# First pair of projection tiles as eight block products, and forget-rank products between the products of a pair

## The chip, the core and the metric

The kernel runs on one core of a Trainium2 chip. The metric is the time of one execution on the device in microseconds (us), the median of several. The core's engines work in parallel and each takes its instructions in program order: TensorE (PE in the profile, its weight loads PEld), VectorE (DVE), ScalarE (ACT), GpSimd (POOL) and SyncE (SP), which here issues the DMA transfers.

## What is computed

One mixer layer on 1,088 tokens (1,024 of a prompt, 64 of a running stream), width 2,048, all in fp32:

```
u = rms_norm(h, norm_pre)
qa, ka, va, za, qg, kg, vg, zg, lr, ga, gg = split_cols(u @ w_in)
y_a = (banded_attention(qa, ka, va) * silu(za)) @ w_branch_attn
log_a = log_sigmoid(lr @ w_forget_up + b_forget) / GLA_TAU
y_g = (rms_norm(gla_mix(qg, kg, vg, log_a, state), gla_norm) * silu(zg)) @ w_branch_gla
merged = sigmoid(ga + b_a) * y_a + sigmoid(gg + b_g) * y_g
h = h + rms_norm(merged @ w_out, norm_post)
```

The change is in `u @ w_in`. The tokens x are multiplied by `norm_pre`, the products are made of these, and the per-token root (rstd) is multiplied onto the results.

## The kernel before

**Numbers.** An fp32 product is made of three fp32r products: of each operand a "hi" part (a copy in the format fp32r, by ScalarE) and a "lo" part (the rest, raw minus hi, by VectorE) are made, and TensorE adds hi*hi, hi*lo and lo*hi in PSUM.

**The mixing phase.** The columns of `w_in` are 60 tiles of 128 (44 of the projections, 16 of the gates), taken two at a time: 30 pairs on the token group 544 to 1087, then the same 30 on tokens 0 to 543. `n` counts these 60 pairs, and pair 30 is `TURN`, where the token group changes. A pair is a 2x2 block problem (2 tiles, 2 halves of the contraction of 8 blocks of 128 rows, 2 halves of 272 tokens: `GAW`), done by a Strassen-like scheme with 7 products (`N_Q`, `q` 0 to 6) in place of 8, of sums of weight blocks (`sum_weights`, four per pair, VectorE) and of sums of token blocks. A product (`split_product`, L1756) is 24 matmuls of 128x272. The weights' hi parts are made by `hi_mix` (L862) into a ring of 3, their lo parts by `lo_mix` (L1206). The results of the products are taken out of PSUM banks 0 to 2 by ScalarE (`s1`, L906) and VectorE (L1339 to L1403, c11, c12, c21, c22), which signal `s_post`; TensorE waits for that before it writes a bank again. TensorE signals each product by `s_mp`.

**The start.** Before pair 0, a loop over 8 steps `j` handles the tokens: each x transfer brings 2 blocks x 544 tokens (rows of 2,176 bytes). ScalarE squares them (L873, into `lr`, with two slots), and TensorE sums the squares over the partitions (L1786: the squares are the weights, a column of ones is moved, 10 matmuls a step in the program, each shown as two). ScalarE and VectorE scale the four blocks (L875, L1236), VectorE forms the four combinations (L1242 to L1248), and every second step ScalarE makes 7 hi parts (L888) and VectorE 7 lo parts (L1253) of 544 elements. Pair 0 waits for the last of these (`s_tlo`). The roots are made during pair 0: mean (L1274), power -0.5 on GpSimd (L1144), diagonals (L1281), a product that spreads them over partitions (L1749), a copy (L1293).

**Forget-rank products.** `lr_products` (L1766) multiplies tokens by the 16 columns of lr (hi and lo as 32 weight columns), as 80 matmuls of 128x272 into banks 4 and 5, in two sums: of 2 terms for one token half and 3 for the other, each term 16 matmuls. It stands after pair 0 and after `TURN`:

```
            for n in range(MIX):
                for q in range(N_Q):
...
                if n == 0:
                    pe.wait_ge(s_lrlo, 1)
                if n % MIX_PAIRS == 0:
                    lr_products()
```

**Second token group.** In pairs 2 to 9 VectorE also combines the tokens of the other group (`held`, L1376 to L1381) and SP stores them; in pairs 29 and 30 they are loaded again (`load_held`) and split by ScalarE (L919) and VectorE (`lo_held`, L1300), between that pair's own work. After the mixing phase come forget gates, late gates with attention and linear attention between their products, the branch products and the output products; nothing there is touched by the change. SP issues all transfers in one queue, in the order written (`load_mix`, `x_first`, `store_mix`, `x_second`, `store_held`).

## Time and profile before

| | |
|---|---|
| median of 3 runs | 2900.48 us (2900.36 to 2903.83) |
| the profiled execution | 2900.14 us, of which the span is 2898.4 us |
| TensorE busy | 2792.8 us, 96% |
| VectorE busy | 1990.5 us, 69% |
| ScalarE busy | 1164.4 us, 40% |
| TensorE clock granted, mean | 0.992 of full |

In the profile, the engine lines give time in which an instruction ran. In the timeline a row has a start in us, how long it ran, engine, line and operation, what it wrote and read (buffer numbers left out), how often, and in brackets the idle time before it and what ended it. Matmuls overlap: the distance of two starts is what one costs the stream, the duration contains its way through the array.

### The profile page before, as it was taken

What the parts mean: (1) busy time and instruction counts of PE and PEld (TensorE: products, weight loads), DVE (VectorE), ACT (ScalarE), POOL (GpSimd) and SP (SyncE); (2) the same over time, 40 slices, a digit from 0 to 9 for tenths busy, and PEclk for the clock granted to TensorE, in tenths of its full rate; (3) what the DMA queues carried; (4) which work ended last, traced back from release to release, by engine and by line L of the source; (5) the groups of instructions that cost most, each with busy time, mean ns of one, the idle gap of its engine ahead of it and who ended that gap; (6) DMA issues with size and microseconds to landing.
All of it is one profiled execution on the core that took longest, in us unless ns stands there. A gap on an engine that the chain in (4) does not pass through costs nothing.

```text
span 2898.4 us, 51546 instructions
## 1 busy us (share of the span) xinstructions
PE 2792.8 (96%) x20490; PEld 2654.8 (92%) x20490; DVE 1990.5 (69%) x3171; ACT 1164.4 (40%) x1908; POOL 80.7 (3%) x55
## 2 busy tenths in 40 slices
PE   6999999999899999999999999999899999999996
PEld 6999999999899999999777887877799999999996
DVE  6799777777788777777777777787543333555555
ACT  5333333344354333344566566565420000343331
POOL 0122000000000000000000000000000000000001
PEclk9999999999999999999999999999999999999998
DMA  3455333435344343433656665565553333555564
GB/s 120 133 182 189 128 129 118 133 125 202 113 133 134 126 130 120 130 122 126 190 176 180 181 188 173 163 195 162 183 169 114 116 115 125 177 179 190 182 192 142
DMA packets 227619, 441.00 MB, mean 152 GB/s; under 512 B 24272, under 2 KB 135120, under 8 KB 226528
## 3 DMA queue, kind: packets, MB, share of 16 engines
q1 hardware_dynamic: 227424, 438.31, 47.4%
q8 instruction: 134, 2.20, 0.3%
q14 instruction: 61, 0.50, 0.0%
HBM read 358.10 MB, written 80.67 MB: 151 GB/s over the span
## 4 chain that ended last, share of the span: by engine, by line
PE 38%; issue 6%; DVE 4%; DMA 2%; ACT 2%; POOL 0%; SPq 0%; POOLq 0%; ACTq 0%; DVEq 0%
PE bank L1734 31%; PE bank L1931 1%; PE bank L1892 1%; DVE w_lo L1185 1%; PE bank L1951 1%; PE bank L1875 1%; PE bank L1956 1%; PE bank L1958 1%; DMA ring<-o_scratch 1%; DVE s L1452 1%; PE bank L1862 1%; ACT w_hi L839 1%; PE bank L1910 0%; DMA ring<-m_scratch 0%; DVE bl L1562 0%
## 5 line engine op out<-in xcount | busy, mean ns | idle before, releaser
L1756 PE MATMUL bank<-th,w_hi 128*128 128x272 f32 x2400 | 699.1, 291 | 14.5 <-DVE w_lo L1206 7.8
L1756 PE MATMUL bank<-tl,w_hi 128*128 128x272 f32 x2400 | 694.1, 289 | 0.0
L1756 PE MATMUL bank<-th,w_lo 128*128 128x272 f32 x2400 | 693.6, 289 | 0.0
L839 ACT ACTIVATE w_hi<-w_raw 128x1024 fp32r<-128x1024 f32 x256 | 270.7, 1058 | 677.6 <-PE bank L1734 638.8
L1185 DVE TENSOR_TENSOR w_lo<-w_raw,w_hi 128x1024 fp32r<-128x1024 f32 x256 | 313.2, 1223 | 250.9 <-ACT w_hi L839 250.5
L1756 PEld LDWEIGHTS bank<-th,w_hi 128*128 128x128 f32 x2400 | 452.7, 189 | 19.8 <-DVE w_lo L1206 10.8
L1756 PEld LDWEIGHTS bank<-tl,w_hi 128*128 128x128 f32 x2400 | 452.8, 189 | 1.0 <-issue 1.0
L1756 PEld LDWEIGHTS bank<-th,w_lo 128*128 128x128 f32 x2400 | 452.3, 188 | 0.0
L862 ACT ACTIVATE w_hi<-w_more 128x1024 fp32r<-128x1024 f32 x240 | 254.6, 1061 | 475.5 <-DVE w_more L1225 255.2
L1206 DVE TENSOR_TENSOR w_lo<-w_more,w_hi 128x1024 fp32r<-128x1024 f32 x240 | 301.4, 1256 | 125.3 <-ACT w_hi L862 123.0
L1734 PE MATMUL bank<-uh,w_hi 128*128 128x272 f32 x1024 | 316.0, 309 | 11.3 <-DVE w_lo L1185 6.4
L1734 PE MATMUL bank<-uh,w_lo 128*128 128x272 f32 x1024 | 295.9, 289 | 0.0
L1734 PE MATMUL bank<-ul,w_hi 128*128 128x272 f32 x1024 | 295.5, 289 | 0.0
L1756 PE MATMUL bank<-uh,w_hi 128*128 128x272 f32 x960 | 280.8, 292 | 5.0 <-ACT stage L906 4.4
L1756 PE MATMUL bank<-ul,w_hi 128*128 128x272 f32 x960 | 279.5, 291 | 0.0
L1756 PE MATMUL bank<-uh,w_lo 128*128 128x272 f32 x960 | 279.0, 291 | 0.0
L862 ACT ACTIVATE w_hi<-w_raw 128x1024 fp32r<-128x1024 f32 x180 | 189.7, 1054 | 195.6 <-PE bank L1756 194.8
L1734 PE MATMUL bank<-bh,w_hi 128*128 128x362 f32 (+1 forms) x768 | 253.7, 330 | 9.0 <-DVE bl L1562 6.8
L1734 PE MATMUL bank<-mh,w_hi 128*128 128x362 f32 (+1 forms) x768 | 252.4, 329 | 1.7 <-DVE ml L1191 1.7
L1734 PE MATMUL bank<-bh,w_lo 128*128 128x362 f32 (+1 forms) x768 | 252.8, 329 | 0.0
L1734 PE MATMUL bank<-bl,w_hi 128*128 128x362 f32 (+1 forms) x768 | 252.6, 329 | 0.0
L1734 PE MATMUL bank<-mh,w_lo 128*128 128x362 f32 (+1 forms) x768 | 252.1, 328 | 0.0
(205 smaller groups left out, 4999.7 us busy)
## 6 DMA issues: line engine op xcount, KB each, us to landing
w_raw<-in_w_tiles SPq DMA_DIRECT2D x376, 512.0 KB, 4.0
w_more<-in_w_tiles SPq DMA_DIRECT2D x120, 512.0 KB, 3.3
p_scratch<-stage SPq DMA_DIRECT2D x44, 544.0 KB, 3.0
gate<-gate_scratch SPq DMA_DIRECT2D x32, 544.0 KB, 4.0
gl<-p_scratch SPq DMA_DIRECT2D x24, 512.0 KB, 5.2
gate_scratch<-stage SPq DMA_DIRECT2D x16, 544.0 KB, 3.0
gate_scratch<-stage SPq DMA_DIRECT2D x64, 136.0 KB, 4.0
o_scratch<-ob SPq DMA_DIRECT2D x16, 512.0 KB, 5.2
```

The source lines that it names most:

```text
L839: act.activation(w_hi[:, h], w_raw[:, h], ACT.Copy).then_inc(s_whi, 1)
L862: act.activation(ring_hi[done % RING], w_src_of[RAW_OF[q]], ACT.Copy).then_inc(s_phi, 1)
L1185: dve.tensor_tensor(w_lo[:, h], w_raw[:, h], w_hi[:, h].bitcast(f32), ALU.subtract).then_inc(s_wlo, 1)
L1206: dve.tensor_tensor(ring_lo[done % RING], w_src_of[RAW_OF[q]], ring_hi[done % RING].bitcast(f32), ALU.subtract).then_inc(s_plo, 1)
L1452: ins = dve.tensor_tensor_reduce(out=s8[0:nq, u % 2, i, 1 + lo:1 + hi], in0=bank[u % 2][0:nq, :].rearrange("p (i k) -> p i k", i=2)[:, i, ...
L1734: ins = pe.matmul(out[:, 0:w], wt[:, h, k, :], ut[:, h * HK + k, 0:w], start=start and k == 0 and j == 0, stop=stop and k == HK - 1 and j ...
L1756: ins = pe.matmul(out[:, 0:GAW], wt[:, k], ut[:, k], start=start and k == 0 and i == 0, stop=stop and k == HK - 1 and i == 2, skip_group_c ...
L1862: ins = pe.transpose(dst[0:nk[kt], kt, i, 0:nq], pb[0:nq, u % 4, i, 1 + kt * P:1 + kt * P + nk[kt]], ident[0:nq, 0:nq])
L1875: ins = pe.matmul(bank[half][0:nq, :].rearrange("p (i k) -> p i k", i=2)[:, i, c0:P + nq], qa[r, tile + i, 0:nq], kw[r, tile // 4, c0:P + ...
L1892: ins = pe.matmul(bank[3][half * HEAD_DIM:(half + 1) * HEAD_DIM, :].rearrange("p (j q) -> p j q", j=GROUP)[:, :, 0:nq], v[0:nk[kt], g * HE ...
L1931: ins = pe.matmul(bank[4][r, l * CHUNK:(l + 1) * CHUNK], k, q, start=True, stop=True)
L1951: ins = pe.matmul(bank[(5, 1)[c]][:, 0:GLA_DV], kt_tok[r, hh], vg[r, v], start=True, stop=True)
```

## The change

It replaces the start and pair 0, moves parts of pair 1's preparation, and moves the forget-rank products.

- Pair 0 is made of eight plain block products (`FIRST`, `first_product`), of two weight tiles x two contraction halves x two token halves, each needing only one raw weight block and one raw token block. Results land in banks 0 to 3, one per quarter.
- x comes as eight transfers of 4 blocks x 272 tokens (rows of 1,088 bytes). A token block is scaled (VectorE three, ScalarE one), and its hi and lo parts are made in halves of 1,088 elements.
- Squares go in 16 pieces into four slots of two blocks; `first_ones` sums a piece by two fp32 matmuls with 64 columns of ones as weights and the squares moved (128x272), one into partitions 0 to 63, one into 64 to 127 of bank 6 or 7. They stand between the block products. After the last, ScalarE copies both banks to `lr` and a `token_sums` (5 matmuls of one column) finishes the sum; the root chain then follows, behind pair 0 and no longer within it.
- The four token combinations are made after the block parts (`sum_blocks`), their hi and lo parts (`hi_sum`, `lo_sum`) partly between pair 1's weight parts.
- `lr_products` is cut up: the two terms of the first sum behind pair 0 (in `TURN` after q=2), two terms of the second after q=4 and the third after q=6 of pair 1 and of `TURN`.

The diff's core:

```
--- before.py
+++ after.py
@@ -43,7 +43,14 @@
-X_FIRST = 5
+FIRST_BLOCKS = ((0, 0), (0, 1), (1, 0), (1, 1))
+FIRST = ((0, 0), (1, 0), (0, 1), (1, 1), (2, 2), (2, 3), (3, 2), (3, 3))
+FIRST_SUMS = (1, 3, 4, 5)
+TOK = 16
+LR_AT = (1, TURN)
...
-                if n > 0:
+                if n == 1:
+                    sp.wait_ge(s_plo, (4, 6, 5, 7)[what])
+                elif n > 1:
                     if what == 0:
-                        sp.wait_ge(s_sum, 4 * (n - 1) + 3)
+                        sp.wait_ge(s_sum, 4 * (n - 2) + 3)
                     else:
                         sp.wait_ge(s_plo, N_Q * (n - 1) + (7, 4, 6)[what - 1])
                 sp.dma_start(w_src_of[slot], w_src(row, h)).then_inc(s_wr[what], 16)
 
+            def x_first(b, half):
+
+                kh, th = FIRST_BLOCKS[b]
+                k, a = kh * HK + 4 * half, MIX_GROUPS[0] * MIX_W + th * GAW
+                sp.dma_start(x_block[b][half], x_view[:, k:k + 4, a:a + GAW]).then_inc(s_x[2 * b + half], 16)
+
+            x_first(0, 0)
+            x_first(0, 1)
             load_mix(0, 0)
-            x_first(2)
-            x_first(3)
             load_mix(0, 2)
+            x_first(1, 0)
+            x_first(1, 1)
+            x_first(2, 0)
+            x_first(2, 1)
+            load_mix(0, 1)
+            x_first(3, 0)
+            x_first(3, 1)
             load_mix(0, 3)
-            x_first(4)
-            x_first(5)
-            load_mix(0, 1)
-            x_first(6)
-            x_first(7)
...
+            def hi_first(e):
+
+                act.wait_ge(s_wr[(0, 2, 1, 3)[e]], 16)
+                ge(act, s_mp, e + 1 if e == 3 else 0)
+                act.activation(ring_hi[(3 + e) % RING], w_src_of[(0, 2, 1, 3)[e]], ACT.Copy).then_inc(s_phi, 4 if e == 0 else 1)
+
+            def squares(*pieces):
+
+                for i in pieces:
+                    b, k = i // 4, 2 * (i % 4)
+                    act.wait_ge(s_x[2 * b + k // 4], 16)
+                    ge(act, s_psq, i - 3)
+                    act.activation(sq_slot[i % 4], x_block[b][k // 4][:, k % 4:k % 4 + 2], ACT.Square).then_inc(s_sq1, 1)
+
+            def hi_block(b):
+
+                for half in range(2):
+                    c = slice(4 * half, 4 * half + 4)
+                    if b == 2:
+                        act.wait_ge(s_xa1, half + 1)
+                    else:
+                        act.wait_ge(s_xgd, 2 * (0, 1, None, 2)[b] + half + 1)
+                    act.activation(block_hi[b][:, c], scaled_block[b][:, c], ACT.Copy).then_inc(s_thi, 1)
+
+            def hi_sum(i):
+
+                q = FIRST_SUMS[i]
+                for half in range(2):
+                    c = slice(4 * half, 4 * half + 4)
+                    act.wait_ge(s_tt, (4, 2, 0, 6)[i] + half + 1)
+                    act.activation(tok_hi[q][:, c], tok_raw[q][:, c], ACT.Copy).then_inc(s_thi, 1)
+
+            squares(0, 1)
+            hi_block(0)
+            hi_first(0)
+            hi_first(1)
+            squares(2, 3, 4, 5)
+            hi_block(1)
+            for half in range(2):
+                act.wait_ge(s_x[4 + half], 16)
+                for k in range(4 * half, 4 * half + 4):
+                    ins = act.activation(scaled_block[2][:, k], x_block[2][half][:, k % 4], ACT.Copy, scale=pre(HK + k))
                 ins.then_inc(s_xa1, 1)
+            hi_block(2)
+            hi_first(2)
+            squares(6, 7)
+            hi_block(3)
+            hi_first(3)
+            squares(*range(8, 16))
+            act.wait_ge(s_sq1, 16)
+            hi_sum(0)
+            act.wait_ge(s_psq, 16)
+            for half in range(2):
+                act.activation(lr[:, half * GAW:(half + 1) * GAW], bank[6 + half][:, 0:GAW], ACT.Copy).then_inc(s_sqc, 1)
+            hi_mix(1, 0)
+            hi_sum(1)
+            hi_sum(2)
+            hi_mix(1, 1)
...
+            def scale_block(b):
+
+                for half in range(2):
+                    dve.wait_ge(s_x[2 * b + half], 16)
+                    for k in range(4 * half, 4 * half + 4):
+                        ins = dve.tensor_scalar(scaled_block[b][:, k], x_block[b][half][:, k % 4], pre(FIRST_BLOCKS[b][0] * HK + k), None, ALU.mult)
+                    ins.then_inc(s_xgd, 1)
+
+            def lo_block(b):
+
+                for half in range(2):
+                    c = slice(4 * half, 4 * half + 4)
+                    dve.wait_ge(s_thi, 2 * b + half + 1)
+                    dve.tensor_tensor(block_lo[b][:, c], scaled_block[b][:, c], block_hi[b][:, c].bitcast(f32), ALU.subtract).then_inc(s_tlo, 1)
+            def lo_first(e):
+
+                dve.wait_ge(s_phi, 4 + e)
+                dve.tensor_tensor(ring_lo[(3 + e) % RING], w_src_of[(0, 2, 1, 3)[e]], ring_hi[(3 + e) % RING].bitcast(f32),
+                                  ALU.subtract).then_inc(s_plo, 4 if e == 0 else 1)
...
+            def lo_sum(i):
+
+                q = FIRST_SUMS[i]
+                for half in range(2):
+                    c = slice(4 * half, 4 * half + 4)
+                    dve.wait_ge(s_thi, 8 + 2 * i + half + 1)
+                    dve.tensor_tensor(tok_lo[q][:, c], tok_raw[q][:, c], tok_hi[q][:, c].bitcast(f32), ALU.subtract).then_inc(s_tlo, 1)
+
+            scale_block(0)
+            lo_block(0)
+            lo_first(0)
+            lo_first(1)
+            scale_block(1)
+            lo_block(1)
+            scale_block(3)
+            lo_block(2)
+            lo_first(2)
+            lo_block(3)
+            lo_first(3)
+            b11, b12, b21, b22 = scaled_block
+            dve.wait_ge(s_xgd, 6)
+            sum_blocks(b11, b12, b11)
+            sum_blocks(b12, b22, b12)
+            dve.wait_ge(s_tt, 2)
+            sum_blocks(b22, b22, b11)
+            dve.wait_ge(s_mp, 5)
+            dve.wait_ge(s_tt, 6)
+            dve.wait_ge(s_xa1, 2)
+            sum_blocks(tok_raw[5], b21, b22)
...
-            for n in range(MIX):
+            lo_mix(1, 0)
+            lo_sum(0)
+            mean_squares(0, MIX_W, bank[5], HEAD_DIM)
+            root_diagonals(0, MIX_W)
+            sum_weights(1, 1)
+            sum_weights(1, 2)
+            lo_mix(1, 1)
+            first = MIX_GROUPS[0] * MIX_W
+            spread(0, MIX_W, bank[6:8], rstd[:, first:first + MIX_W])
+            dve.wait_ge(s_rstd, 2)
+            for i, (m, half) in enumerate(((0, 0), (0, 1), (1, 0), (1, 1))):
+                dve.wait_ge(s_mp, 6 + m)
+                ins = dve.tensor_tensor(c_out[:, m, half * GAW:(half + 1) * GAW], bank[i][:, 0:GAW],
+                                        rstd[:, first + half * GAW:first + (half + 1) * GAW], ALU.mult)
+                if i < 3:
+                    ins.then_inc(s_post, (2, 3, 1)[i])
+                else:
+                    ins.then_inc(s_cm, 3)
+
...
+                if n == 1:
+                    lo_sum(1)
...
-            def lr_products():
-
-                for i, terms in enumerate((((0, 0), (1, 2)), ((0, 4), (0, 0), (1, 6)))):
...
+            def lr_products(i, which):
+
+                terms = LR_TERMS[i]
+                for n in which:
+                    kh, q = terms[n]
+                    for k in range(HK):
+                        for j, ut in enumerate((tok_hi[q], tok_lo[q])):
+                            ins = pe.matmul(bank[4 + i][0:2 * RANK, 0:GAW], wlr[:, kh * HK + k, :], ut[:, k],
+                                            start=n == 0 and k == 0 and j == 0, stop=n == len(terms) - 1 and k == HK - 1 and j == 1)
+                if which[-1] == len(terms) - 1:
                     ins.then_inc(s_lrp, 1)
...
+            def first_ones(*pieces):
+
+                for i in pieces:
+                    th = FIRST_BLOCKS[i // 4][1]
+                    pe.wait_ge(s_sq1, i + 1)
+                    for j in range(2):
+                        ins = pe.matmul(bank[6 + th][j * HEAD_DIM:(j + 1) * HEAD_DIM, 0:GAW], ones[:, 0:HEAD_DIM], sq_slot[i % 4][:, j],
+                                        start=i in (0, 4), stop=i in (11, 15), skip_group_check=True)
+                    ins.then_inc(s_psq, 1)
+
+            def first_product(n):
+
+                e, b = FIRST[n]
+                pe.wait_ge(s_plo, 4 + e)
+                hi_w, lo_w = ring_hi[(3 + e) % RING], ring_lo[(3 + e) % RING]
+                for k in range(HK):
+                    if k % 4 == 0:
+                        pe.wait_ge(s_tlo, 2 * b + k // 4 + 1)
+                    for i, (wt, ut) in enumerate(((hi_w, block_hi[b]), (hi_w, block_lo[b]), (lo_w, block_hi[b]))):
+                        ins = pe.matmul(bank[2 * (e % 2) + FIRST_BLOCKS[b][1]][:, 0:GAW], wt[:, k], ut[:, k], start=e < 2 and k == 0 and i == 0,
+                                        stop=e >= 2 and k == HK - 1 and i == 2, skip_group_check=True)
+                if FIRST_BLOCKS[b][1] == 1:
+                    ins.then_inc(s_mp, 4 if e == 0 else 1)
+
             pe.wait_ge(s_cset, 1)
-            for j in range(HK):
...
-            for n in range(MIX):
+            for n, pieces in enumerate(((0, 1), (2, 3), (4, 5), (), (), (6, 7), (8, 9, 10, 11), (12, 13, 14, 15))):
+                first_ones(*pieces)
+                first_product(n)
+            pe.wait_ge(s_sqc, 2)
+            token_sums(MIX_W, bank[5], lr)
+            pe.wait_ge(s_lrlo, 1)
+            lr_products(0, (0, 1))
+            spread_roots(0, MIX_W, bank[6:8])
+
+            for n in range(1, MIX):
                 for q in range(N_Q):
                     pe.wait_ge(s_plo, N_Q * n + q + 1)
-                    if n == 0:
-                        pe.wait_ge(s_tlo, 3 * N_Q + q + 1)
+                    if n == 1 and q in FIRST_SUMS:
+                        pe.wait_ge(s_tlo, 8 + 2 * FIRST_SUMS.index(q) + 2)
                     if n == TURN:
-                        pe.wait_ge(s_tlo, 4 * N_Q + q + 1)
+                        pe.wait_ge(s_tlo, TOK + q + 1)
...
-                if n % MIX_PAIRS == 0:
-                    lr_products()
+                    if n == TURN and q == 2:
+                        lr_products(0, (0, 1))
+                    if n in LR_AT and q == 4:
+                        lr_products(1, (0, 1))
+                    if n in LR_AT and q == 6:
+                        lr_products(1, (2,))
```

ScalarE at the start of the program, before (in program order; `lr` holds the squares, `ul_raw` and `tl_raw` the scaled and combined tokens, `uh` and `th` hi parts):

```order
L873 ACTIVATE lr<-stage 128x544 x2
L875 ACTIVATE ul_raw<-stage,norm_sb 128x272 x2
L862 ACTIVATE w_hi<-w_raw 128x1024
L873 ACTIVATE lr<-stage 128x544 x2
L875 ACTIVATE ul_raw<-stage,norm_sb 128x272 x2
L888 ACTIVATE uh<-ul_raw 128x544
L888 ACTIVATE th<-tl_raw 128x544
```

And in the changed kernel (`th_raw` and `stage` hold x, `tl_raw` and `xs` the scaled blocks):

```order
L898 ACTIVATE lr<-th_raw 128x544 x2
L908 ACTIVATE uh<-tl_raw 128x1088 x2
L890 ACTIVATE w_hi<-w_raw 128x1024
L890 ACTIVATE w_hi<-w_more 128x1024
L898 ACTIVATE ring<-th_raw 128x544 x2
L898 ACTIVATE lr<-th_raw 128x544 x2
L908 ACTIVATE th<-tl_raw 128x1088 x2
L927 ACTIVATE xs<-stage,norm_sb 128x272 x8
L908 ACTIVATE uh<-xs 128x1088 x2
L890 ACTIVATE w_hi<-w_raw 128x1024
```

One block's hi parts and the first two weights now stand right behind the first two squares; before, seven hi parts came after the second transfer and this was repeated four times.

VectorE around the roots, before (`mean` is the mean square, `ring<-ident,root` the diagonals, `rows` the spread roots, `stage` results):

```order
L1274 TENSOR_SCALAR mean<-bank 128x4
L1275 TENSOR_SCALAR mean<-bank 32x1
L1227 TENSOR_TENSOR w_more<-w_raw,w_more 128x1024
L1206 TENSOR_TENSOR w_lo<-w_raw,w_hi 128x1024
L1230 TENSOR_TENSOR w_raw<-w_raw,w_more 128x1024
L1281 TENSOR_SCALAR ring<-ident,root 128x128 x4
L1281 TENSOR_SCALAR ring<-ident,root 32x128
L1206 TENSOR_TENSOR w_lo<-w_more,w_hi 128x1024
L1339 TENSOR_TENSOR stage<-stage,bank 128x272
L1206 TENSOR_TENSOR w_lo<-w_more,w_hi 128x1024
L1293 COPY rows<-bank 128x512
```

And in the changed kernel:

```order
L1355 TENSOR_SCALAR mean<-bank 128x4
L1356 TENSOR_SCALAR mean<-bank 32x1
L1362 TENSOR_SCALAR ring<-ident,root 128x128 x4
L1362 TENSOR_SCALAR ring<-ident,root 32x128
L1277 TENSOR_TENSOR w_more<-w_more 128x1024
L1281 TENSOR_TENSOR w_more<-w_more,w_raw 128x1024
L1262 TENSOR_TENSOR w_lo<-w_more,w_hi 128x1024
L1374 COPY rows<-bank 128x512
L1374 COPY rows<-bank 128x32
L1398 TENSOR_TENSOR stage<-bank,rows 128x272 x4
```

The diagonals stand directly behind the mean, with nothing between them, and two weight sums and one weight rest of pair 1 stand between the diagonals and the copy of the spread roots.

TensorE in `TURN`, at the end of q=2, before (the product of q=3 follows at once):

```order
L1756 MATMUL bank<-uh,w_hi 128x272
L1756 MATMUL bank<-ul,w_hi 128x272
L1756 MATMUL bank<-uh,w_lo 128x272
L1756 MATMUL bank<-th,w_hi 128x272
L1756 MATMUL bank<-tl,w_hi 128x272
```

And in the changed kernel:

```order
L1855 MATMUL bank<-uh,w_hi 128x272
L1855 MATMUL bank<-ul,w_hi 128x272
L1855 MATMUL bank<-uh,w_lo 128x272
L1868 MATMUL bank<-uh,wlr 32x272
L1868 MATMUL bank<-ul,wlr 32x272
```

Thirty-two matmuls of the forget rank now stand between the products of q=2 and q=3, 32 more behind q=4 and 16 behind q=6; before, all 80 stood behind q=6.

## Rows read from the trace of the kernel before

**Rows 1.** The page, busy time of each engine (share of the span) and instructions:

```profile
PE 2792.8 (96%) x20490; PEld 2654.8 (92%) x20490; DVE 1990.5 (69%) x3171; ACT 1164.4 (40%) x1908; POOL 80.7 (3%) x55
```

**Rows 2.** Windows: length, PE, PEld, DVE, ACT, POOL busy, PEclk, DMA, GB/s:

```profile
20.00:40.00 20.00, 13.71 (x68) 13.46 (x68) 14.02 (x25) 13.29 (x25) 0.00 (x0) 1.00 0.17 46
40.00:60.00 20.00, 16.33 (x80) 16.03 (x81) 17.26 (x32) 13.15 (x24) 1.77 (x1) 1.00 0.00 1
60.00:80.00 20.00, 20.00 (x159) 19.74 (x158) 16.10 (x25) 5.91 (x7) 2.52 (x1) 1.00 0.32 107
```

**Rows 3.** Timeline of TensorE, the start:

```profile
34.32 8.03 PE L1786 MATMUL bank<-ones,lr 128*128 128x1 f32 x40 [3.07 <-ACT lr L873]
45.43 8.03 PE L1786 MATMUL bank<-ones,lr 128*128 128x1 f32 x40 [3.08 <-ACT lr L873]
54.06 0.57 PE L1756 MATMUL bank<-uh,w_hi 128*128 128x272 f32 x1 [0.60 <-DVE ul L1253]
...
59.63 0.32 PE L1756 MATMUL bank<-th,w_hi 128*128 128x272 f32 x1
```

**Rows 4.** Timeline of TensorE, end of pair 0 to first product of pair 2:

```profile
79.26 0.29 PE L1766 MATMUL bank<-uh,wlr 128*32 128x272 f32 x1
...
89.21 0.29 PE L1756 MATMUL bank<-uh,w_hi 128*128 128x272 f32 x1
...
110.40 0.29 PE L1756 MATMUL bank<-uh,w_hi 128*128 128x272 f32 x1
```

**Rows 5.** Timeline of TensorE in `TURN`, q=2 to the first product of pair 31:

```profile
734.32 0.56 PE L1756 MATMUL bank<-uh,w_hi 128*128 128x272 f32 x1 [4.41 <-ACT stage L906]
...
738.98 0.28 PE L1756 MATMUL bank<-uh,w_lo 128*128 128x272 f32 x1
...
741.46 0.36 PE L1756 MATMUL bank<-th,w_hi 128*128 128x272 f32 x1 [1.82 <-DVE stage L1339]
...
746.07 0.29 PE L1756 MATMUL bank<-th,w_hi 128*128 128x272 f32 x1
...
765.09 0.29 PE L1756 MATMUL bank<-uh,w_hi 128*128 128x272 f32 x1
```

**Rows 6.** Timeline of VectorE in `TURN`, the take-out for which q=3 waits:

```profile
738.55 2.42 DVE L1300 TENSOR_TENSOR tl<-tl_raw,th 128x2176 fp32r<-128x2176 f32 x1
740.88 0.43 DVE L1339 TENSOR_TENSOR stage<-stage,bank 128x272 f32<-128x272 f32 x1
```

**Rows 7.** Timeline of ScalarE, the start:

```profile
5.99 1.20 ACT L873 ACTIVATE lr<-stage 128x544 f32<-128x544 f32 x2 [1.20 <-DMA stage<-in_xT]
7.10 0.92 ACT L875 ACTIVATE ul_raw<-stage,norm_sb 128x272 f32<-128x272 f32 x2
8.84 1.06 ACT L862 ACTIVATE w_hi<-w_raw 128x1024 fp32r<-128x1024 f32 x1 [0.82 <-DMA w_raw<-in_w_tiles]
...
12.37 0.66 ACT L888 ACTIVATE uh<-ul_raw 128x544 fp32r<-128x544 f32 x1
```

**Rows 8.** Timeline of VectorE, the start and the roots of pair 0:

```profile
7.32 0.64 DVE L1236 TENSOR_SCALAR tl_raw<-stage,norm_sb 128x272 f32<-128x272 f32 x2 [0.67 <-DMA stage<-in_xT]
...
21.44 1.22 DVE L1206 TENSOR_TENSOR w_lo<-w_raw,w_hi 128x1024 fp32r<-128x1024 f32 x1
...
62.56 1.06 DVE L1281 TENSOR_SCALAR ring<-ident,root 128x128 f32<-128x128 f32 x5 [1.08 <-POOL root L1144]
...
67.16 0.79 DVE L1293 COPY rows<-bank 128x512 f32<-128x512 f32 x2 [0.92 <-PE bank L1749]
67.98 0.44 DVE L1361 TENSOR_TENSOR stage<-bank,rows 128x272 f32<-128x272 f32 x1
```

**Rows 9.** Timeline of TensorE, fp32 products with 128 and with 64 weight columns:

```profile
789.33 1.88 PE L1779 MATMUL bank<-wup,lr 128*128 128x512 f32 x4
...
1435.72 0.43 PE L1958 MATMUL bank<-st,qb 128*64 128x256 f32 x1
1435.73 0.43 PE L1963 MATMUL bank<-st,qb 128*64 128x256 f32 x1
...
1436.30 0.39 PE L1734 MATMUL bank<-uh,w_hi 128*128 128x272 f32 x1
```

**Rows 10.** Timeline of GpSimd, the power -0.5 of pair 0:

```profile
58.23 4.30 POOL L1144 TENSOR_TENSOR root<-mean,minus_half 128x5 f32<-128x5 f32 x1 [56.85 <-DVE mean L1275]
```

172 lines of the change are left out of this document (56 added, 116 removed).

## The prediction

> **What bounds the kernel now.** I read the page first: TensorE is busy for 2792.8 us of the span, VectorE for 1990.5 [rows 1], so time can come only from where TensorE waits or works for nothing. The windows by stage show one such place at once [rows 2]: in 20 to 40 and 40 to 60 us it has 68 and 80 instructions in 13.7 and 16.3 us, against 159 in the full window after. The timeline says what they are [rows 3]: forty short products at a time of the sum of squares, with idle time between that ScalarE ends, in a cycle of 45.43 - 34.32 = 11.1 us, four times. The first product of pair 0 starts at 54.06. The start is therefore bound by ScalarE and VectorE, which split all seven token operands before the first product may run, and TensorE's 8 us of sums in each cycle stand in ScalarE's way.
>
> From there on TensorE is nearly full. Two numbers set the scale: a product of 24 matmuls takes 3.03 us (seven in the 21.19 us from 89.21 to 110.40, [rows 4]), 0.126 us a matmul, and the 80 forget-rank matmuls take 89.21 - 79.26 = 9.95 us, 0.124 each [rows 4]. The first product took 59.63 - 54.06 = 5.57 us [rows 3], 0.23 a matmul: this is the lower of the two clock levels (1.2 GHz), after a stretch of waits and one-column work, although the window's mean still prints 1.00. The second hole is in `TURN` [rows 5]: TensorE waits 4.41 us before q=2 and 1.82 us before q=3, the latter for a take-out that VectorE can do only behind a 2.42 us token rest [rows 6].
>
> **The change, step by step.** The common mark is the first product of pair 2, at 110.40 before [rows 4]; behind it the order is the same until `TURN`.
>
> *To the first block product.* The first x transfer is there at 5.99 [rows 7], the second at 7.32 [rows 8]; with shorter rows I put it at 7.7, and weight 0 at 9.0 (8.8 before, [rows 7]), weight 2 at 10.3. ScalarE: two squares 1.2, two hi halves of 1,088 elements at 1.07 (1,024 take 1.06, 544 take 0.66, [rows 7]) with the second waiting for VectorE's scaling of the second transfer (4 x 0.3 = 1.2, to 8.9), so until 10.1; weight 0 until 11.0. VectorE: lo halves at 1.2 until 11.3, the weight's rest 1.13 (1.22 less overlap, [rows 8]): 12.5. The first block product starts at **12.5** instead of 54.06.
>
> *Pair 0.* From 12.5 on, TensorE has eight products, 8 x 3.03 = 24.2 us (one more than before: +3.0), and 14 of the 16 pieces of squares. A piece is two fp32 products of 272 columns. Four records of 512 columns take 1.88 us [rows 9], so one product is two records, 0.94 us per 512 columns and 0.50 per 272. Two products that write different partition halves start 0.01 us apart and with their second records are through in 1436.30 - 1435.72 = 0.58 us for 256 columns [rows 9]: they run side by side. (The Trainium skill, "TensorE: Matmul & The Clock Gate", Part 3, says that a weight load overlaps a running matmul only when the row group differs. Both products here use all rows, so by that page the pairs would run one behind the other, which is the first rival below; these rows disagree with it.) I take 0.5 for a piece, 7.0 for the 14 (bounds 0.45 and 0.6: -0.7, +1.4). The clock starts at its lower level again; as at 54.06 I give it 5.6 us of that, a loss of 2.8 (bounds 1.5 and 4). Nothing else is late: counting on, VectorE has the last weight's rest at 29.7 and ScalarE the last hi part at 28, when TensorE is in its fifth product; the squares' four slots are then freed by TensorE itself. Pair 0 ends at 12.5 + 24.2 + 7.0 + 2.8 = **46.5**.
>
> *From pair 0 to pair 1.* This is new: pair 1 writes banks 0 to 3, which VectorE takes out with the roots, and the roots come last. The last piece is summed at 46.5 - 3.0 = 43.5. Then ScalarE's two copies 0.8 (with 0.2 to start), a weight 1.0, VectorE's weight rest 1.1 and two token rests 2.4: 49.0; TensorE's own end of the sum is done by 47.5. Mean 0.15, the power 4.30 on GpSimd [rows 10], diagonals 1.06 [rows 8], two weight sums 2.3, ScalarE's copy 1.05, the rest 1.15, the copies of the roots 0.8 and the first take-out 0.4 [rows 8], 0.2 to TensorE: **60.4**. TensorE fills 4.0 us of this with 32 forget-rank matmuls and 1.4 with the spreading; it idles about 3 us before and 3 us after that.
>
> *Pair 1.* Seven products 21.2, 48 forget-rank matmuls 6.0. After the idle time the clock may be at its lower level: after 4.41 us of idle in `TURN` it stayed there from 734.32 to 738.98 [rows 5], which costs half of 4.66, 2.3. I take that (bounds 0 and 3). VectorE's work in pair 1 (four take-outs, four weight sums, seven weight rests, three token rests, the memsets of `lr`) adds up to 26 us, under TensorE's 29.5, so it is covered, with 3 us in hand. Pair 2 starts at 60.4 + 21.2 + 6.0 + 2.3 = **89.9**. Gain so far: 110.4 - 89.9 = **20.5**.
>
> *Transfers.* The same bytes as before; pair 1's weights are asked for when pair 0's rests are done, from 12.5 on, 40 us before use. The one store of pair 0 has 10 us until c11 of pair 1. SP's queue has nothing else near. Cost nothing; if that cover went, it would be a wait of one transfer, some 3 us.
>
> *`TURN`.* The 32 matmuls (4.0 us) behind q=2 fall where TensorE now waits for VectorE [rows 5, 6]. q=2 ends at 739.6, they end at 743.6, and q=3 starts there instead of at 741.46. From there four products and 48 matmuls: 743.6 + 12.1 + 6.0 = 761.7, against 765.09 before: 3.4 gained, if the second slow stretch (q=3 took 746.07 - 741.46 = 4.6 us, 1.6 more than 3.03) does not come when TensorE no longer pauses; 1.8 if it comes all the same. Bounds 0 (VectorE still late) and 3.4. I take 2.9, nearer the upper, since the pause that stands before the slow stretch is what is filled.
>
> **Sum:** 20.5 + 2.9 = 23.4 us. The profiled execution took 2900.14; the median of the runs is 0.34 above it. 2900.48 - 23.4 = **2877.0 us**.
>
> **Rivals.**
>
> *The squares' products run one after the other.* In a pair the two products have the same weights and rows, and the program gives both records of the first before those of the second. Then a piece is 2 x 0.50 less overlap, 0.91, and the 14 cost 5.7 us more: 2882.7. Against it stand the two starts 0.01 us apart [rows 9], which also had all 128 rows. Chance 0.15.
>
> *VectorE bounds pair 1.* Its 26 us against 29.5 is a small reserve; with 0.1 us more at each of some 25 handovers it is gone, and if the clock is not low there it is exceeded: +3 us, 2880. This lies inside the forecast's range.
>
> *The early start is mostly lost again.* If TensorE's first product only gets its operands after a full round of splitting, or the root chain is held by one more wait such as the constants (`s_const`, whose transfers are behind all x), pair 1 starts around 75 and the gain is some 6 to 9: 2893. Against it: every operand of the chain was counted and the constants land by 30. Chance 0.03. That the `TURN` part does nothing gives 2880, also inside the range.
>
> *Slower: the clock does not rise.* TensorE in the start ran 8.0 us at a time on sums without rising [rows 3]; in the new start fp32r products and fp32 sums alternate. If it stays at the lower level through pairs 0 and 1, pair 0 takes 8 x 5.5 + 14 x 1.0 = 58 us from 12.5 to 70, the chain ends at 82, pair 1 takes 49 and ends at 131: 20.6 later than before, less 2.9: 2918. It decides from some 57 us at the lower level on (23.4 / 0.5 on top of the 10 that the sum holds). Against it: the product at 54.06 raised the clock within 5.57 us. Chance 0.03.
>
> **How the numbers follow.** Forecast 0.79, serial squares 0.15, mostly lost 0.03, slower 0.03. Low end: all clock and square terms at their good bound, 2877.0 - 0.7 - 1.3 - 2.3 - 0.5 is 2872.2; I take 2871. High end: serial squares plus VectorE's 2.5, about 2885. What a measurement of this kernel can tell from no change is 0.2%, 5.8 us: faster means under 2894.7, which all but the last case are (with some of the lost-again case near the line). Faster 0.95, within 0.2% 0.02, slower 0.03.
>
> **What would show it.** First block product at 12 to 13 us; pair 0's last at 45 to 48; a piece of squares 0.5 and not 0.9 apart at the full clock; first product of pair 1 at 59 to 62 with its wait ended by VectorE's take-out; pair 2 at 88 to 92; in `TURN`, no idle before q=3, and pair 31 some 22 us behind q=2's end (25.5 before). Wrong would be: TensorE waits of over 1 us inside pair 0 ended by ScalarE or VectorE, waits in pair 1 ended by a weight or token rest, a slow stretch over 8 us.

## The result, and the profile after

The changed kernel takes 2870.43 us (median of 4 runs, 2866.53 to 2872.04) against 2901.56 for the kernel before: ratio 0.989, interval 0.9873 to 0.9907. Over all runs, the later ones included, the medians are 2870.21 (12 runs) and 2901.60 (42 runs), 31.4 us apart, or 1.08%. The prediction was 2877.0, with 2871 as its low end, so the measured time lies just outside the range. The direction was right, and so were the two places where a gain was forecast; the gain is 31.1 us where the sum had 23.4, and part of it came in a place for which the sum had nothing. The profiled execution is the fastest of its four, 2866.53 us, with a span of 2864.6.

The page, busy time of each engine. TensorE has 62 instructions fewer than in [rows 1], as the program has it (24 more for the eighth product, 74 instead of 160 for the sums of squares):

```profile
PE 2774.1 (97%) x20428; PEld 2632.0 (92%) x20428; DVE 1978.8 (69%) x3147; ACT 1157.3 (40%) x1886; POOL 79.2 (3%) x55
```

Windows by stage (length, then busy time of PE, PEld, DVE, ACT, POOL, granted clock, DMA share, GB/s), to be held against [rows 2]:

```profile
20.00:40.00 20.00, 20.00 (x156) 17.46 (x155) 19.36 (x25) 12.61 (x18) 0.00 (x0) 1.00 0.43 151
40.00:60.00 20.00, 15.39 (x115) 13.57 (x114) 12.34 (x21) 10.87 (x13) 1.18 (x1) 0.92 0.04 17
60.00:80.00 20.00, 20.00 (x160) 19.47 (x160) 18.89 (x21) 5.60 (x6) 0.00 (x0) 0.99 0.36 110
```

TensorE is full from 20 us on; the hole is now one wait in 40 to 60. Its timeline, first at the start, then from the end of pair 0 to pair 2:

```profile
12.26 0.59 PE L1903 MATMUL bank<-uh,w_hi 128*128 128x272 f32 x1 [3.77 <-DVE w_lo L1306]
...
17.07 1.14 PE L1890 MATMUL bank<-ring,ones 128*64 128x272 f32 x8
18.14 0.39 PE L1903 MATMUL bank<-uh,w_hi 128*128 128x272 f32 x1
...
46.31 1.10 PE L1841 MATMUL bank<-ones,lr 128*128 128x1 f32 x10
...
57.35 0.56 PE L1855 MATMUL bank<-uh,w_hi 128*128 128x272 f32 x1 [4.61 <-DVE stage L1398]
...
61.73 0.29 PE L1855 MATMUL bank<-th,w_hi 128*128 128x272 f32 x1
...
85.89 0.29 PE L1855 MATMUL bank<-uh,w_hi 128*128 128x272 f32 x1
```

The first block product takes 17.07 - 12.26 = 4.8 us instead of 3.03: until 15.83 its matmuls are 0.23 us apart, the distance at the lower clock level, and 0.126 from then on (the granted clock prints 1.00 here all the same, as it did at 54.06 before). The two pieces of squares behind it take 1.07 us. Pair 1 starts at 57.35 and its first product takes 61.73 - 57.35 = 4.38, at a granted clock of 0.67 on average. Why pair 1 starts 3 us before its forecast stands on GpSimd, against the 4.30 us of [rows 10]:

```profile
48.88 1.18 POOL L1200 TENSOR_TENSOR root<-mean,minus_half 128x5 f32<-128x5 f32 x1 [47.51 <-DVE mean L1356]
```

In `TURN`, against [rows 5]: q=1 (698.88), q=2 (706.58), q=3 (713.71) and the first product of pair 31:

```profile
698.88 0.60 PE L1855 MATMUL bank<-th,w_hi 128*128 128x272 f32 x1 [3.02 <-DVE w_lo L1262]
...
706.58 0.36 PE L1855 MATMUL bank<-uh,w_hi 128*128 128x272 f32 x1 [3.05 <-ACT stage L959]
...
713.71 0.36 PE L1855 MATMUL bank<-th,w_hi 128*128 128x272 f32 x1
...
731.88 0.29 PE L1855 MATMUL bank<-uh,w_hi 128*128 128x272 f32 x1
```

The wait before q=3 is gone; those before q=1 and q=2 stay.

The first products of pairs 2, 9, 29 and 31 cut the program into stretches that can be compared between all profiles. Below, the gain of each is from the profiles of kernels that are alike in it (before: 2 to 3 profiles, after: 3):

| stretch | before, us | after, us | gain | predicted |
|---|---|---|---|---|
| start to pair 2 | 110.40, 110.04 | 85.89, 86.20, 86.73 | 23.9 | 20.5 |
| pairs 2 to 8 | 155.77, 154.74, 154.57 | 153.33, 153.39, 153.30 | 1.7 | 0 |
| pairs 9 to 28 | 428.68 to 428.72 | 428.68 to 428.70 | 0 | 0 |
| pairs 29 and 30 (`TURN`) | 70.24, 71.17 | 63.96, 66.38, 66.73 | 5.0 | 2.9 |

Together 30.6 us. Three of the four rows exceed their forecast and need a cause that the prediction did not have. The row of `TURN` is the least sure: it rests on two profiles of the kernel before, and the section on the turn narrows it.

### The profile page after: what moved, and what is told of

It reads as the page before. It is cut to its first block and busy times, and to the rows that moved or that the text cites. A ratio compares the mean times of both kernels' runs of the same rounds, so it can differ in the third digit from the quotient of the medians.

```text
span 2864.6 us, 51375 instructions
## 1 busy us (share of the span) xinstructions
PE 2774.1 (97%) x20428; PEld 2632.0 (92%) x20428; DVE 1978.8 (69%) x3147; ACT 1157.3 (40%) x1886; POOL 79.2 (3%) x55
## 5 line engine op out<-in xcount | busy, mean ns | idle before, releaser
L1855 PE MATMUL bank<-th,w_hi 128*128 128x272 f32 x2360 | 687.3, 291 | 10.2 <-DVE w_lo L1262 7.1
L1855 PE MATMUL bank<-tl,w_hi 128*128 128x272 f32 x2360 | 682.5, 289 | 0.0
L1855 PE MATMUL bank<-th,w_lo 128*128 128x272 f32 x2360 | 681.9, 289 | 0.0
L1855 PEld LDWEIGHTS bank<-th,w_hi 128*128 128x128 f32 x2360 | 445.0, 189 | 14.8 <-DVE w_lo L1262 8.6
L1855 PEld LDWEIGHTS bank<-tl,w_hi 128*128 128x128 f32 x2360 | 445.1, 189 | 1.0 <-issue 1.0
L1855 PEld LDWEIGHTS bank<-th,w_lo 128*128 128x128 f32 x2360 | 444.6, 188 | 0.0
L1262 DVE TENSOR_TENSOR w_lo<-w_more,w_hi 128x1024 fp32r<-128x1024 f32 x236 | 295.2, 1251 | 110.5 <-ACT w_hi L880 108.2
```

What stands on the lines that cost most here:

```text
L1262: dve.tensor_tensor(ring_lo[done % RING], w_src_of[RAW_OF[q]], ring_hi[done % RING].bitcast(f32), ALU.subtract).then_inc(s_plo, 1)
L1855: ins = pe.matmul(out[:, 0:GAW], wt[:, k], ut[:, k], start=start and k == 0 and i == 0, stop=stop and k == HK - 1 and i == 2, skip_group_c ...
```

## The experiments

Single runs of one kernel scatter by about 2 us (the 12 of the changed kernel lie between 2866.17 and 2873.39), so medians of four are some 1.5 us sure. The marks in the profile are sharper, outside `TURN` and up to pair 31; behind it, where the change touches nothing, the executions of the study took between 2132.2 and 2137.9 us for the same work (time of the execution less its mark).

### How stable the gain is

The changed kernel was run twice more. The texts on record for the two:

> The changed kernel once more, nothing edited: it tells how much of the result is the same in every execution. Theory (sizes off, mechanism right): its gain over the kernel before is 31 to 34 us wherever it is run, because the terms that came out larger than predicted are structural (the power on GpSimd 3.1 us shorter, pairs 3 to 8 2.4 us, the turn 2.5 us). Rival (luck of the clock): the gain swings by more than 4 us from run to run and its middle lies near the 23.4 us of the prediction, about 2877.

> The changed kernel again, on the same chip as the three that follow, to measure them against. Its median should be 2868 to 2871 us as in the two runs before. In the profile, the first block product and the first product of pair 1 should again take 4.3 to 5.4 us instead of 3.03, behind waits of 3.4 and 4.6 us.

Measured: 2868.71 (2867.46 to 2871.02) and 2871.94 (2866.17 to 2873.39), ratios 0.9889 and 0.9898. The gains over the kernel before on the same chip are 31.1, 32.2 and 28.6 us. The last is under the 31 to 34 of the theory, but the middle is at 31 and not near 23.4, so luck of one execution does not explain the miss. The third profile's first block product took 5.5 us, a little over the 5.4 expected, and pair 1's first product 4.7. The swing sits in `TURN`: 63.96, 66.38 and 66.73 us. In the profile of the first of them both q=1 and q=2 were slow there (4.6 and 5.6 us), in the one shown above only q=1.

### The turn alone, from both sides

In the changed kernel all 80 matmuls go back behind q=6 of `TURN`:

```diff
-                    if n == TURN and q == 2:
+                    if n == TURN and q == 6:
                         lr_products(0, (0, 1))
-                    if n in LR_AT and q == 4:
-                    if n in LR_AT and q == 4:
+                        lr_products(1, (0, 1, 2))
+                    if n == 1 and q == 4:
                         lr_products(1, (0, 1))
-                    if n in LR_AT and q == 6:
+                    if n == 1 and q == 6:
                         lr_products(1, (2,))
```

> The changed kernel with all 80 forget-rank matmuls of TURN behind the last product again; the start as changed. Theory: the turn's part of the gain is what the trace gives for pairs 29 and 30, up to 5.5 us, so this is 3 to 5.5 us slower than the changed kernel, with idle time before q=3 of TURN back (1 to 2 us). Rival (as predicted): 2.9 us or less. Rival (the turn gives nothing, clock luck only): within 1 us of the changed kernel.

Measured: 2871.17 us (2869.88 to 2874.32), 2.5 more than the changed kernel on the same chip, and the wait before q=3 is back (1.35 us). Then the kernel before with `lr_products` split as in the change, and nothing else:

```diff
...
+                    if n == TURN and q == 2:
+                        lr_products(0, (0, 1))
+                    if n == TURN and q == 4:
+                        lr_products(1, (0, 1))
+                    if n == TURN and q == 6:
+                        lr_products(1, (2,))
                 if n == 0:
                     pe.wait_ge(s_lrlo, 1)
-                if n % MIX_PAIRS == 0:
-                    lr_products()
+                    lr_products(0, (0, 1))
+                    lr_products(1, (0, 1, 2))
```

> The kernel before with only the turn's part of the change: 32 forget-rank matmuls behind q=2 of TURN, 32 behind q=4, 16 behind q=6. Theory: 3 to 5.5 us faster than the kernel before, the same step as between the first experiment and the changed kernel with the sign turned; no wait before q=3. As predicted: 2.9 faster (2897.6). Rival (the turn gives nothing): within 1 us.

Measured: 2897.94 us (11 runs), 3.0 less than before, ratio 0.999 (0.9981 to 0.9999). By the times the turn is worth 2.5 to 3.0, as predicted; by the marks its stretch went from 70.7 to 64.87 (5.8) in this kernel and from 68.49 to 65.7 (2.8) in the other. The spread between these is the slow products: one execution has none to two more than another.

The stretch can be cut more finely. Up to the last matmul of q=2 all these kernels do the same work, and only behind it do they differ. In the profile of the changed kernel that matmul starts at 709.54 and pair 31 at 731.88, in the kernel before at 739.35 and 765.09. Over all profiles of kernels that are alike here:

| from the last matmul of q=2 to pair 31 | us |
|---|---|
| split as in the change (8 profiles) | 22.20 to 22.56, mean 22.36 |
| all 80 behind q=6 (4 profiles) | 23.90, 23.91, 25.74, 28.67, mean 25.55 |

So the move itself gives 3.2 us on average, close to the 2.9 of the prediction. The split form takes the same time in every profile; the form before does not. It takes 23.9 where q=3 is fast in spite of its wait, 25.7 and 28.7 where q=3 is slow (behind waits of 1.82 and 3.87 us). What the stretch shows ahead of this point (41.5 to 45.0 us) is the same program in all of them, and differs by chance. Not every slow product costs time: q=2 starts 7.7 us behind q=1's start in all twelve, whether q=1 took 3.1 us (and TensorE waited 4.4) or 4.5 (and it waited 3.0), since ScalarE's take-out ends that wait either way.

### The power on GpSimd

The changed kernel, with VectorE's weight sums beside the power:

```diff
-            root_diagonals(0, MIX_W)
             sum_weights(1, 1)
             sum_weights(1, 2)
+            root_diagonals(0, MIX_W)
```

> The changed kernel with VectorE's two sums of pair 1's weights (1,024 elements each, 1.2 us) before the root diagonals instead of behind them, so that they run beside GpSimd's power. Theory (contention): GpSimd's power of five columns takes 4 us beside VectorE's long operations and 1.18 us alone, so it goes from 1.18 back to 3 to 4.3 us, and the weight sums may take longer than 1.2 too; the diagonals then come at about 52.5 to 53 and are done some 1.5 us later against 2.3 us of sums saved behind them: pair 1 starts within 1 us of where it does now, total within 1.5 us. Rival (the 4.30 us was the price of the first power in its place, or chance): the power stays at 1.18 and pair 1 starts 1 to 1.2 us earlier.

GpSimd and VectorE in it:

```profile
49.45 2.03 POOL L1200 TENSOR_TENSOR root<-mean,minus_half 128x5 f32<-128x5 f32 x1 [48.09 <-DVE mean L1356]
```

```profile
49.23 1.20 DVE L1277 TENSOR_TENSOR w_more<-w_more 128x1024 f32<-128x1024 f32 x1
50.96 1.23 DVE L1281 TENSOR_TENSOR w_more<-w_more,w_raw 128x1024 f32<-128x1024 f32 x1 [0.52 <-DVE w_more L1277]
```

And the reverse in the kernel before: the diagonals right behind the means, so that VectorE waits.

```diff
+                if n == 0:
+                    root_diagonals(0, MIX_W)
                 sum_weights(n, 3)
...
-                if n == 0:
-                    root_diagonals(0, MIX_W)
```

> The kernel before with the root diagonals of pair 0 directly behind the means, so that VectorE waits while GpSimd takes the power; the weight sums that ran beside it follow. Theory (contention): the power at about 58 us takes 1.18 us instead of 4.30. Rival (another cause): it stays at about 4.3. The time of the whole should move by less than 1.5 us either way.

```profile
58.43 1.18 POOL L1144 TENSOR_TENSOR root<-mean,minus_half 128x5 f32<-128x5 f32 x1 [57.06 <-DVE mean L1275]
```

Beside the 4.30 us of [rows 10], VectorE in the kernel before (the power from 58.23 to 62.53):

```profile
58.01 1.20 DVE L1227 TENSOR_TENSOR w_more<-w_raw,w_more 128x1024 f32<-128x1024 f32 x1
59.14 1.20 DVE L1206 TENSOR_TENSOR w_lo<-w_raw,w_hi 128x1024 fp32r<-128x1024 f32 x1
60.27 1.21 DVE L1230 TENSOR_TENSOR w_raw<-w_raw,w_more 128x1024 f32<-128x1024 f32 x1
```

The same power takes 1.18 us with VectorE idle, in both kernels, 2.03 behind one sum of 1.20, and 4.30 behind three operations in a row, which end at 60.27 + 1.21 = 61.48. It ends 51.48 - 50.43 = 1.05 us after the one, and 62.53 - 61.48 = 1.05 after the three. I read this as GpSimd's work not getting slower but starting when VectorE pauses. The pause can be short: the second sum of e3_beside_pow reads what the first wrote, and the gap between the two, 52.40 - 52.30 = 0.10 us in the changed kernel with GpSimd idle, is 50.96 - 50.43 = 0.53 here. It looks as if the power went in between and held VectorE for some 0.4 us. The two sums in the changed kernel:

```profile
51.09 1.21 DVE L1277 TENSOR_TENSOR w_more<-w_more 128x1024 f32<-128x1024 f32 x1
52.40 1.23 DVE L1281 TENSOR_TENSOR w_more<-w_more,w_raw 128x1024 f32<-128x1024 f32 x1
```

The three operations of the kernel before overlap by 0.07 us each and left it no such gap. (The Trainium skill, "SBUF — State Buffer", section "Who interferes with whom", says that a VectorE instruction with two inputs in SBUF contends with a GpSimd instruction that reads SBUF, that the contention is an exclusive lock, and, of VectorE's modes that use both ports, that the one that issues first keeps the ports for its whole instruction while the other is fully blocked. The rows with one sum agree. Those with three differ in one point: the power was held through two operations that VectorE began after the power.) The size I expected for one sum, 3 to 4.3, was too large. Nor did pair 1 start where it did: it started at 56.20, 1.15 earlier, as the rival had it (but the rival's power of 1.18 did not come), since two sums of 2.3 us are saved behind the diagonals for 0.85 of waiting. That kernel takes 2866.1 us (2863.14 to 2870.22), 4.1 under all runs of the changed kernel, where a difference within 1.5 was expected; pair 1's first product, now behind a wait of 1.50 us, takes 3.10 instead of 4.38. The kernel with the idle power has one execution, 2902.41 us, which tells nothing of its time.

### Whether the squares' products run side by side

```diff
-            mean_squares(0, MIX_W, bank[5], HEAD_DIM)
+            mean_squares(0, MIX_W, bank[5], P)
...
-                        ins = pe.matmul(bank[6 + th][j * HEAD_DIM:(j + 1) * HEAD_DIM, 0:GAW], ones[:, 0:HEAD_DIM], sq_slot[i % 4][:, j],
-                                        start=i in (0, 4), stop=i in (11, 15), skip_group_check=True)
+                        ins = pe.matmul(bank[6 + th][:, 0:GAW], ones[:, 0:P], sq_slot[i % 4][:, j],
+                                        start=i in (0, 4) and j == 0, stop=i in (11, 15) and j == 1, skip_group_check=True)
```

> The changed kernel with each product of ones and squares written to all 128 partitions (128 columns of ones instead of 64), so that the two products of a piece add into the same place and cannot run side by side; the mean is scaled by 1/128 of the sum instead of 1/64, and so computes the same. Theory: products that write different partition halves run side by side, 0.5 us a piece; without that a piece takes 0.95 to 1.0 us at the higher clock, pair 0 ends 6 to 8 us later (about 53) and the whole is 5 to 8 us slower than the changed kernel. Rival: the side-by-side running has another cause than the partition halves, or the pieces were not what TensorE waited for: within 1 us.

```profile
11.98 0.39 PE L1903 MATMUL bank<-uh,w_hi 128*128 128x272 f32 x1 [1.46 <-DVE w_lo L1306]
...
15.11 2.00 PE L1890 MATMUL bank<-ring,ones 128*128 128x272 f32 x8
16.74 0.49 PE L1903 MATMUL bank<-uh,w_hi 128*128 128x272 f32 x1
...
35.74 2.00 PE L1890 MATMUL bank<-lr,ones 128*128 128x272 f32 x8
37.57 2.00 PE L1890 MATMUL bank<-ring,ones 128*128 128x272 f32 x8
```

The same four pieces in the changed kernel:

```profile
36.00 1.14 PE L1890 MATMUL bank<-lr,ones 128*64 128x272 f32 x8
36.97 1.09 PE L1890 MATMUL bank<-ring,ones 128*64 128x272 f32 x8
```

Two pieces (8 records) take 37.57 - 35.74 = 1.83 us here and 36.97 - 36.00 = 0.97 in the changed kernel: 0.91 a piece against 0.49, just the two prices of the prediction. So it is the form with 64 columns in two partition halves that runs side by side, and the form with 128 columns in one place does not. The run changes the number of columns and the place together; which of the two decides was not tested. The kernel takes 2873.31 us (2870.66 to 2877.54), only 3.1 more than the changed one and not the 5 to 8 expected, and its pair 0 ends at 49.11, not at 53, because something was won at the same time: the longer pieces keep TensorE busy until 10.5 us, it waits only 1.46, and the first block product takes 3.1 us instead of 4.8. That pointed to the next question.

### What makes a product slow

Useless fp32 products of ones with ones go into TensorE's waits; nothing useful moves:

```diff
+            def warm(count, to):
+
+                for i in range(count):
+                    pe.matmul(bank[to][:, 0:P], ones[:, 0:P], ones[:, 0:P], start=True, stop=True, skip_group_check=True)
...
                 first_ones(*pieces)
+                if n == 0:
+                    warm(12, 4)
...
             spread_roots(0, MIX_W, bank[6:8])
+            warm(14, 5)
...
+                    if (n, q) in ((TURN - 1, 4), (TURN, 0), (TURN, 1)):
+                        warm(8 if q == 4 else 10, 3)
```

> The changed kernel with useless fp32 products of ones with ones (128 columns, result read by nobody) put into TensorE's waits: 12 before the first block product, 14 before pair 1, 8 before q=5 of the pair before TURN, 10 behind q=0 and 10 behind q=1 of TURN. Nothing useful moves. Theory (a product is slow because TensorE waited before it): the first block product and pair 1's first take 3.0 us, as in the runs whose wait before them was 1.5 us, and the slow products at TURN go: 1.8, 1.3 and 1.5 to 4 us, in all 4 to 6 us faster than the changed kernel. Rival (the clock falls for another reason, or the fillers are longer than the waits): the same slow products remain, or each filler delays the product behind it, and the time is the same or up to 2 us more.

```profile
8.90 3.45 PE L1897 MATMUL bank<-ones 128*128 128x128 f32 x24
12.60 0.39 PE L1908 MATMUL bank<-uh,w_hi 128*128 128x272 f32 x1 [0.24 <-DVE w_lo L1306]
...
15.60 0.29 PE L1908 MATMUL bank<-uh,w_lo 128*128 128x272 f32 x1
...
56.09 0.36 PE L1855 MATMUL bank<-uh,w_hi 128*128 128x272 f32 x1 [1.28 <-DVE stage L1398]
...
688.53 0.36 PE L1855 MATMUL bank<-th,w_hi 128*128 128x272 f32 x1 [1.80 <-DVE stage L1494]
...
693.16 0.28 PE L1855 MATMUL bank<-uh,w_hi 128*128 128x272 f32 x1
```

Measured: 2865.42 us (2862.99 to 2865.96), 6.5 less than the changed kernel on the same chip and 4.8 less than all its runs. Both products at the start now run at the 2.4 GHz level (3.0 us each; for pair 1's the granted clock is 1.00, and 0.67 in the changed kernel), and pair 2 starts at 83.34. At these two products the lower level does come from the wait before: with the wait filled it does not occur. In this profile `TURN` gained nothing: its stretch took 65.03 us, inside the 63.96 to 66.73 of the changed kernel, and of the gain the marks show 2.9 us at pair 2 and 3.2 at pair 31. One slow product is left, q=6 of pair 29 at 688.53 (4.6 us), behind a wait of 1.80. Over all profiles of the study up to pair 32: none of the eleven products behind a wait of 1.0 to 1.71 us was slow, of those behind 1.80 to 3.15 some were and some not, and all behind 3.24 and more were. The length of the wait is not all there is: in the kernel before, the product at 54.06 was slow behind a wait of only 0.60 us, but ahead of it stood 8 us of one-column sums and, between these, waits of 3.1 us [rows 3].

### Filling and shortening the waits with useful work

Token 0's forget-rank terms need nothing that is late, so they can stand in the waits of `TURN` and before pair 1:

```diff
-            LR_TERMS = (((0, 0), (1, 2)), ((0, 4), (0, 0), (1, 6)))
+            LR_TERMS = (((0, 0), (1, 2)), ((0, 0), (0, 4), (1, 6)))
...
             spread_roots(0, MIX_W, bank[6:8])
+            lr_products(1, (0,))
...
+                    if n == TURN and q == 0:
+                        lr_products(0, (0,))
+                    if n == TURN and q == 1:
+                        lr_products(1, (0,))
                     if n == TURN and q == 2:
-                        lr_products(0, (0, 1))
+                        lr_products(0, (1,))
                     if n in LR_AT and q == 4:
-                        lr_products(1, (0, 1))
+                        lr_products(1, (1,))
```

> The changed kernel with the terms of the forget-rank products that use only token 0 put where TensorE still waits: 16 matmuls (2.0 us) behind q=0 and 16 behind q=1 of TURN, 16 behind q=2 instead of 32, and 16 of the second sum before pair 1 instead of behind its q=4. The waits there are 3.0, 3.05 and 4.6 us in the trace of the changed kernel. Theory: each of the three moved pieces falls into a wait that VectorE or ScalarE ends, so each gives 2.0 us, less the clock's part: about 6 us faster than the changed kernel (bounds 4 and 8, the upper if the clock then stays at its higher level). Rival: the waits are not bound elsewhere but by a chain that goes through TensorE (a ring slot freed by the product before), so the filler only shifts the wait: 0 to 2 us.

Measured: 2864.65 us (2863.44 to 2867.62), 4.1 less than the changed kernel. The stretch of `TURN` takes 62.17 instead of 63.96 to 66.73. It is the lower bound of what I expected: behind the filler, q=3 waits 0.37 for a take-out of VectorE and the pairs 2 to 8 give 1.1 back (154.39 instead of 153.3), so part of the filled time was owed to VectorE. The 4.1 us lie at the low end of the theory and well above the 0 to 2 of the rival.

VectorE's chain before pair 1 is shortened by moving the sums and a token rest into its idle time:

```diff
-            lo_mix(1, 0)
-            lo_sum(0)
-            mean_squares(0, MIX_W, bank[5], HEAD_DIM)
-            root_diagonals(0, MIX_W)
             sum_weights(1, 1)
             sum_weights(1, 2)
+            lo_sum(0)
+            lo_mix(1, 0)
+            mean_squares(0, MIX_W, bank[5], HEAD_DIM)
+            root_diagonals(0, MIX_W)
             lo_mix(1, 1)
```

(ScalarE has `hi_mix(1, 1)` right behind `hi_mix(1, 0)`.)

> The changed kernel with VectorE's work between pair 0 and pair 1 put in another order: the two sums of pair 1's weights and token 1's rest come first, into VectorE's idle time from 39.7 to 45.0 us, then weight 0's rest, means, diagonals, weight 1's rest; ScalarE splits weight 1 directly behind weight 0. Theory: the chain from the last square to pair 1 loses 2.3 us of weight sums and 1.1 us of waiting for ScalarE; TensorE's own 32 forget-rank matmuls then end at 51.3 before the spreading, so pair 1 starts at 53.5 to 54.5 instead of 57.35 and the whole is 3 us faster than the changed kernel (bounds 2 and 4). Rival: VectorE bounds pair 1, so that what is gained before it is lost in it: within 1 us.

```profile
51.88 1.39 PE L1848 MATMUL bank<-ring,ones 128*128 128x128 f32 x10
54.77 0.36 PE L1855 MATMUL bank<-uh,w_hi 128*128 128x272 f32 x1 [1.50 <-DVE stage L1398]
...
57.87 0.29 PE L1855 MATMUL bank<-th,w_hi 128*128 128x272 f32 x1
```

Pair 1 starts 2.6 us earlier, and its first product, behind a wait of 1.50, takes 3.10 instead of 4.38: pair 2 starts at 82.03, 3.9 earlier. The median is 2865.82 (2861.89 to 2869.34), 4.4 under all runs of the changed kernel, a little more than the 2 to 4 expected. Both edits together, with 16 forget-rank matmuls, the spreading and 32 more before pair 1:

> The early weight sums and the filled waits together: VectorE's order as in e5_early_sums, the token-0 terms at TURN as in e6_fill_waits; before pair 1 TensorE has 16 forget-rank matmuls, the spreading, 16 more, and 16 of the second sum. Theory: the terms add, since they lie in different places: 3 to 4 us (start) and 3 to 4 us (TURN) against the changed kernel, about 2862. TensorE now has no wait of over 1.5 us before pair 1, which starts at 53.5 to 54.5 and runs at the higher clock. Rival: in pair 1 VectorE is now the bound and waits of 0.5 us or more ended by weight rests give 1 to 2 us back: 2864.

Measured: 2859.39 us (2857.45 to 2861.76), ratio 0.9862, 10.8 under all runs of the changed kernel. That is better than the 2862 expected; the marks show 7.6 of it by pair 31 (726.37 against 734.0 on average), the rest lies where the kernels are the same. TensorE waits 1.07 us before the spreading and not at all before pair 1, which runs at the higher clock from its start at 56.24 (expected 53.5 to 54.5: the 48 forget-rank matmuls now fill the time until then); pair 2 starts at 81.43. With useless products in the three waits left:

> The kernel of e7_both with useless products in the three waits that are left: 12 before the first block product, 8 before q=5 of the pair before TURN, 8 behind q=1 of TURN. Theory: 3 to 4 us faster than e7_both, about 2859. Rival: no gain over it.

Measured: 2861.43 (2859.55 to 2865.27), 2.0 more than e7_both on the same chip: no gain, as the rival had it. The start of pair 1 came 1.3 us earlier, and the mark at pair 31 stood where it had (726.62 against 726.37): in `TURN`, q=3 then waited 1.89 for VectorE and was slow. In this execution VectorE, and not TensorE, set the pace there.

### Pairs 2 to 8

From pair 5 on the changed kernel takes 22.34 us for a pair, not 21.20. One of them as a window, and VectorE in the pair ahead of it:

```profile
172.20:194.54 22.34, 21.66 (x170) 21.31 (x169) 20.58 (x25) 8.89 (x10) 6.01 (x3) 1.00 0.57 188
```

```profile
161.30 2.15 DVE L1262 TENSOR_TENSOR w_lo<-w_more,w_hi 128x1024 fp32r<-128x1024 f32 x1 [0.44 <-ACT w_hi L880]
...
163.83 1.17 DVE L1475 TENSOR_TENSOR xs<-xs 128x272 f32<-128x272 f32 x1
164.92 1.60 DVE L1476 TENSOR_TENSOR xs<-xs 128x272 f32<-128x272 f32 x1
166.55 0.44 DVE L1478 TENSOR_TENSOR xs<-xs 128x272 f32<-128x272 f32 x1
```

Beside them GpSimd squares and sums x of the other token group:

```profile
159.61 2.76 POOL L1214 TENSOR_TENSOR ring<-xs 128x1088 f32<-128x1088 f32 x1 [15.74 <-DMA xs<-in_xT]
162.45 3.77 POOL L1217 TENSOR_TENSOR ssq<-ssq,ring 128x544 f32<-128x544 f32 x2
```

VectorE is busy for 20.58 of the 22.34 us and waits 1.6 us for ScalarE's hi parts, and TensorE's one wait in such a pair, before q=1, is ended by VectorE's rest of a weight. For what ScalarE makes of that x it does not wait: the row at 163.83 follows the one before it at once. GpSimd's operations were cut to one column, in the changed kernel and, as a second run, in the kernel before:

```diff
-                pool.tensor_tensor(held_sq, held_x, held_x, ALU.mult).then_inc(s_ssq, 1)
+                pool.tensor_tensor(held_sq[:, :, 0:1], held_x[:, :, 0:1], held_x[:, :, 0:1], ALU.mult).then_inc(s_ssq, 1)
...
-                    pool.tensor_tensor(ssq[:], ssq[:], held_sq[:, kh], ALU.add).then_inc(s_ssq, 1)
+                    pool.tensor_tensor(ssq[:, 0:1], ssq[:, 0:1], held_sq[:, kh, 0:1], ALU.add).then_inc(s_ssq, 1)
```

> The changed kernel with GpSimd's squares of the second half of x and their sums cut from 1,088 and 544 columns to one column each (that part of the computation is left out). Theory: pairs 5 to 8 take 22.34 us each, not 21.2, because VectorE bounds them, and VectorE is slow there because GpSimd's operations beside it lengthen its own (2.15 instead of 1.22 us, 1.17 and 1.60 instead of 0.44). Without them pairs 2 to 8 take 7 x 21.2 = 148.4 us instead of 153.3: about 4.9 us faster than the changed kernel. Rival: those pairs are bound by the transfers of the held x or by ScalarE's chain: the pairs stay at 22.3.

> The same cut in the kernel before (that part of the computation is left out). Theory: pairs 2 to 8 took 155.8 us there; the cut brings them to 148.4 too, so this is 6 to 7.4 us faster than the kernel before, and the 1 to 2.4 us that the changed kernel gained in these pairs are gone between this run and the one above it. Rival: the pairs of the kernel before were slow for another reason (SP's queue order), and a difference of 1 us or more between the two stays.

VectorE's operations in e10_light_after, the same as above:

```profile
160.62 1.23 DVE L1262 TENSOR_TENSOR w_lo<-w_more,w_hi 128x1024 fp32r<-128x1024 f32 x1 [0.72 <-ACT w_hi L880]
...
162.86 0.43 DVE L1475 TENSOR_TENSOR xs<-xs 128x272 f32<-128x272 f32 x1
163.21 0.44 DVE L1476 TENSOR_TENSOR xs<-xs 128x272 f32<-128x272 f32 x1
```

And one pair of each:

```profile
150.18:171.39 21.21, 21.21 (x171) 21.21 (x169) 17.91 (x24) 9.00 (x11) 1.40 (x3) 1.00 0.60 197
```

```profile
151.97:173.17 21.20, 21.20 (x171) 21.20 (x169) 17.90 (x24) 9.00 (x11) 1.09 (x3) 1.00 0.62 197
```

Pairs 2 to 8 take 148.43 us in both, and the difference between the kernels is gone. GpSimd's work cost VectorE 20.58 - 17.91 = 2.7 us a pair, and that made VectorE the bound; the rivals (the transfers, ScalarE, SP's queue order) would have left the pairs at 22.3 or a difference between the kernels. The times: 2862.09 us (2861.84 to 2864.56), 8.1 under the changed kernel's runs, and 2890.35 (2887.07 to 2892.16), 11 to 13 under the kernel before. Both are more than expected (4.9, and 6 to 7.4). Pairs 9 and 10, at 22.35 and 22.19 us in the changed kernel, fall to 21.2 as well (pairs 9 to 28: 426.55 instead of 428.70), which is 2.1 of it; the rest, 1 us in the one and 2.5 to 4 in the other, was not traced further and is of the size by which executions differ at the start and from `TURN` on. Where the changed kernel's 1.7 us lay shows mostly in pair 4: 21.5 us in its three profiles, 22.33 to 23.11 in the three of the kernel before. I read this as VectorE coming into these pairs with a larger lead and using it up one pair later. No run varied the lead alone, but the kernel with the filled waits fits: it takes 16 matmuls, 2.0 us, away from TensorE in pair 1, its pair 4 takes 22.33 us, and 1.1 of the 1.7 us are gone.

Then the same work off GpSimd with the result kept, on top of the kernel of e7_both: squares by ScalarE, their sums by VectorE.

```diff
+                        act.activation(held_sq, held_x, ACT.Square).then_inc(s_xg2, 1)
...
-                pool.tensor_tensor(held_sq, held_x, held_x, ALU.mult).then_inc(s_ssq, 1)
...
+                        dve.tensor_tensor(ssq[:], ssq[:], held_sq[:, kh], ALU.add).then_inc(s_ssq, 1)
```

> The kernel of e7_both with the held squares on ScalarE (1,088 columns, about 1.1 us a pair) and their two sums on VectorE (544 columns, about 0.72 us each, from 0.43 for 272), nothing on GpSimd. Theory: VectorE pays 1.4 us a pair and is spared the 2.8 us that GpSimd's operations cost it, so its cycle falls from 22.34 to 21.0 and TensorE bounds the pairs at 21.2: 4 to 6 us faster than e7_both, about 2854. Rival: what VectorE saves it pays, or ScalarE's square comes late and holds VectorE: within 1 us of e7_both.

> The kernel above with the 12 useless products before the first block product. Theory: the first block product takes 3.0 instead of 4.9 us, less what the fillers delay it (0.3 to 0.6): 1.3 us faster than the kernel above, as between the first product of pair 1 in e8_both_warm (54.93) and e7_both (56.24). Rival: no difference, because what is gained before pair 1 is a wait for VectorE later.

```profile
145.90:167.66 21.76, 21.55 (x171) 21.29 (x169) 19.23 (x27) 10.01 (x11) 0.00 (x0) 1.00 0.59 194
```

The row is one pair of the first. Its time is 2858.55 us (2856.07 to 2860.54), that of the second 2856.24 (2854.92 to 2858.97), ratio 0.9838 (0.9824 to 0.9851), the fastest kernel of the study, 14 us below the changed one. A pair takes 21.75, not 21.2: VectorE still ends the waits, 0.2 us at a time, though it is busy for only 19.23 us; the rest of its cycle are waits of its own, 1.6 us of them for ScalarE. Why this comes to 21.75 was not tested. To the start of pair 29 the move gives 4.0 us (660.54 against 664.55), but in `TURN` 1.5 of them went again, and the median moved by only 0.8 between two chips, or by 3.4 if each is held against the kernel before on its own chip. The 4 to 6 us of the expectation were not reached, and by the times alone the gain is not clear of the scatter. The useless products before the first block product gave 1.6 us to pair 1 (54.38 against 56.02), and pair 29 still started 1.6 earlier.

## Where the prediction failed, and what of it held

The step that failed is in the chain of the roots: "the power 4.30 on GpSimd [rows 10]". It took 1.18 us, and pair 1 started 3 us early. A second term was put at nothing without a reason: "behind it the order is the same until `TURN`", where 1.7 us were gained. The prediction's structure held, and part of its agreement is luck. Term by term:

- *First block product at 12.5.* It came at 12.26.
- *Pair 0 ends at 46.5.* It ended at 46.31, but two errors of 1.0 us cancel here. The loss to the clock was 1.8 and not 2.8, and the 14 pieces of squares with their handovers took 8.0 us and not 7.0. A piece costs 0.49 where two pairs of pieces follow each other, as taken. The rival of serial squares would have been 0.91, and is ruled out for this form by the run that made it so. (The prediction took from the Trainium skill, "TensorE: Matmul & The Clock Gate", Part 3, only the rule on weight loads, and said that by that page the pairs would run one behind the other. The same part also lists products in different column tiles of the array as running side by side, so the page, read whole, does not speak for that rival, and the 0.49 us agree with it.)
- *Root chain to 60.4.* Pair 1 started at 57.35. The power began at 48.88 (0.3 earlier than counted), took 3.1 us less, and the way from its end to pair 1 was 7.3 us and not 6.95. The duration of 4.30 was right for its row and wrong for the new place, where VectorE no longer works beside it. The lists of program order ahead of the prediction had it: between the mean and the diagonals stand three operations of VectorE in the kernel before and nothing in the changed one.
- *Pair 1's clock loss 2.3.* It was 1.35 (1.5 and 1.6 in the two other profiles): the term was mis-sized within its bounds. With the 3.05 us by which pair 1 came early this makes the 4 us that pair 2 came early in the profiled execution (85.89, predicted 89.9).
- *Nothing between pair 2 and `TURN`.* The order is the same there, as the prediction said, but I took TensorE for the bound, and did not ask why pairs took 22.34 us in one place and 21.20 in another.
- *`TURN` 2.9.* This term held: behind the last matmul of q=2 the move gives 3.2 us on average, by the times 2.5 and 3.0, and the forecast mark, pair 31 some 22 us behind q=2's end, was met. What I had wrong is that the time before is not one number: 25.5 us was what one execution took, others take 24 to 28.5. The 5.0 of the table comes from that.
- *VectorE bounds pair 1* did not happen, nor did the clock stay low.

The table's excess over the forecast is 3.4 + 1.7 + 2.1 = 7.2 us. The first is the power and pair 1's clock, less what the start of the other profiles gave back; the second is pairs 2 to 8; the third is mostly the scatter of two profiles of the kernel before. That VectorE sets the power's duration is shown by runs that lift it and bring part of it back; that it is worth 3.1 us at pair 1 is read from the chain, and no run gave the changed kernel a power of 4.3. That GpSimd makes pairs 4 to 10 long is shown by the runs that took its work away. With 3.2 us for `TURN` the places add up to 28.8 of the 31.1 to 31.4 us; where the other 2 to 3 us lie is open.

## What to carry to other kernels

A duration of GpSimd or VectorE taken from a trace belongs to what the other of the two did at that time: look at both timelines over the row before you move it, and keep GpSimd's passes over data away from a stretch where VectorE is near its limit. A wait of TensorE can cost more than its length, since the product behind it may run at half the clock (and does cost more unless the next wait takes that up); work that needs nothing late belongs there. And when one engine is 96% busy, still compare the period of each stage with its smallest one: 22.34 against 21.20 us showed the second bound.

## What was not expected of the hardware

- The power of five columns on GpSimd took 1.18, 2.03 and 4.30 us behind none, one and three VectorE operations that followed each other without a gap: it waited for the whole run, not only for the operation in progress. A gap between two operations seems to let it in, and then VectorE waited some 0.4 us.
- In the other direction, GpSimd's operations on 1,088 and 544 columns stretch VectorE's from 1.22 to 2.15 and from 0.44 to 1.17 and 1.60 us.
- The lower clock level came behind a wait of only 1.80 us in one execution and did not come behind 3.15 in another (e3_beside_pow); what decides between them these runs do not tell.
